# Sums over the key blocks behind: block sums by VectorE, 18 products a head in place of 20

## The reference, cut to what matters

```
z = einsum('bhqd,bhkd->bhqk', q_blk, k32) * scale
mask = key_pos[None, :] < q_pos[:, None]
log_1m_beta = where(mask, log_sigmoid(-z), 0.0)
stick = cumsum(log_1m_beta, axis=3, reverse=True) - log_1m_beta
att = where(mask, exp(log_sigmoid(z) + stick), 0.0)
out = einsum('bhqk,bhkd->bhqd', att, v32)
```

## Time and profile before

| | |
|---|---|
| median of three executions | 1718.95 us |
| profiled execution, its own time | 1719.79 us |
| its span in the profile | 1717.8 us |
| TensorE busy | 1692.4 us, 99% |
| VectorE busy | 1316.4 us, 77% |
| ScalarE busy | 778.2 us, 45% |
| GpSimd busy | 780.0 us, 45% |
| mean granted TensorE clock | 0.998 |

### The profile page before, as it was taken

The page is one execution under the profiler, slowest core; times in us unless marked ns, Lnnn a source line. Parts: engine busy times, 40 slices in busy tenths (PEclk is TensorE's granted clock), DMA queues, the critical chain, the costliest instruction groups (busy, mean ns, idle before and its releaser), DMA issues.

```text
span 1717.8 us, 24432 instructions
## 1 busy us (share of the span) xinstructions
PE 1692.4 (99%) x9073; PEld 1511.4 (88%) x9073; DVE 1316.4 (77%) x1872; ACT 778.2 (45%) x1124; POOL 780.0 (45%) x494
## 2 busy tenths in 40 slices
PE   7999999999999999999999999999999999999998
PEld 6878788878899999999999999999888888888886
DVE  4666622265889999989999777766778888888887
ACT  4445433344333666656666566654323323323233
POOL 4333243333702556655656667770453433433430
PEclk9999999999999999999999999999999999999999
DMA  5222223332335677686776977788999999999992
GB/s 159 74 73 85 61 86 98 89 85 84 111 112 207 233 250 256 232 303 242 245 258 240 346 273 269 271 298 306 378 352 396 383 382 391 380 372 390 385 390 90
DMA packets 212443, 413.88 MB, mean 241 GB/s; under 512 B 11520, under 2 KB 150816, under 8 KB 207008
## 3 DMA queue, kind: packets, MB, share of 16 engines
q1 hardware_dynamic: 156880, 253.51, 42.4%
q0 software_dynamic: 36864, 134.23, 21.4%
q10 hardware_dynamic: 18640, 25.45, 4.2%
HBM read 360.73 MB, written 52.43 MB: 241 GB/s over the span
## 4 chain that ended last, share of the span: by engine, by line
PE 87%; DVE 9%; ACT 2%; issue 1%; DMA 0%; ACTq 0%; SPq 0%; DVEq 0%
PE psum L1371 30%; PE psum L1312 25%; PE psum L284 20%; PE psum L1302 4%; PE psum L1339 2%; DVE ul L1567 2%; DVE ring L1642 1%; PE psum L358 1%; PE psum L512 1%; DVE hot L1630 1%; PE psum L345 1%; PE psum L372 1%; DVE hot L1632 1%; DMA acc<-in_x 0%; PE psum L327 0%
## 5 line engine op out<-in xcount | busy, mean ns | idle before, releaser
L1312 PE MATMUL psum<-xnTh,uh 128*128 128x384 f32 x1024 | 354.2, 346 | 3.4 <-DVE ul L1567 2.6
L1312 PE MATMUL psum<-xnTh,ul 128*128 128x384 f32 x1024 | 343.4, 335 | 0.0
L1312 PE MATMUL psum<-xnTl,uh 128*128 128x384 f32 x1024 | 343.4, 335 | 0.0
L236 POOL TENSOR_TENSOR wl<-raw,wh 128x1024 fp32r<-128x1024 f32 x72 | 177.1, 2465 | 280.4 <-ACT wh L586 279.9
L1371 PE MATMUL psum<-vh,dwh 128*128 128x512 f32 x768 | 298.8, 389 | 0.2 <-DVE dwl L1660 0.2
L1371 PE MATMUL psum<-vh,dwl 128*128 128x512 f32 x768 | 298.8, 389 | 0.0
L1371 PE MATMUL psum<-vl,dwh 128*128 128x512 f32 x768 | 298.8, 389 | 0.0
L1526 POOL DMA_INDIRECT ring<-in_expert_v,index x128 | 172.1, 1345 | 251.7 <-DVE acc L1647 208.1
L1444 ACT ACTIVATE vh<-v_raw 128x4096 fp32r<-128x4096 f32 x31 | 112.7, 3634 | 339.2 <-PE psum L1371 338.7
L1526 POOL DMA_INDIRECT ring<-in_expert_u,index x128 | 169.7, 1326 | 181.0 <-DVE ring L1642 107.8
L1642 DVE SCALAR_TENSOR_TENSOR ring<-ring,x 128x1024 f32<-128x1024 f32 x128 | 197.1, 1559 | 5.0 <-issue 2.9
(11 more groups left out here) (230 smaller groups left out, 3029.3 us busy)
## 6 DMA issues: line engine op xcount, KB each, us to landing
u_raw<-in_expert_u SPq DMA_DIRECT2D x128, 512.0 KB
v_raw<-in_expert_v SPq DMA_DIRECT2D x30, 2048.0 KB, 14.0
expert_act<-hb ACTq DMA_DIRECT2D x128, 192.0 KB
expert_gate<-grid SPq DMA_DIRECT2D x12, 2048.0 KB, 6.9
dh<-expert_act SPq DMA_DIRECT2D x32, 768.0 KB
dg<-expert_gate SPq DMA_DIRECT2D x32, 768.0 KB
raw<-in_w_in SPq DMA_DIRECT2D x40, 512.0 KB, 3.9
raw<-in_w_q SPq DMA_DIRECT2D x16, 512.0 KB, 4.0
```

Of the source, the lines that this page charges most:

```text
L236: nc.gpsimd.tensor_tensor(wl[slot][:], raw[slot][:], wh[slot][:].bitcast(F), ALU.subtract).then_inc(w_lo[slot], 1)
L1312: last = nc.tensor.matmul(zb[s][:, 0:DT], w[s][:, c, :], x[:, c, 0:DT], start=(c == 0 and i == 0), stop=(c == C - 1 and i == 2))
```

## The change

For each head VectorE adds three blocks: `sx[0]` is key block 2 plus key block 3 for the queries of block 3, `sx[1]` is key block 1 plus key block 2 for the queries of block 2, and `sx[2]` is key block 1 plus `sx[0]` for the queries of block 3. ScalarE copies the high part of these 384 columns (`sxh`), and VectorE subtracts the low part (`sxl`). TensorE multiplies the block right behind a key block by ones as before, and what lies further behind as one product on the summed blocks. The counts of the semaphore `vmax` go from one to three for each head.

```diff
+    sx = m.put("sx", 84, [P, 2, 3, P])
+    sxh = m.put("sxh", 87, [P, 2, 3, P], R)
+    sxl = m.put("sxl", 90, [P, 2, 3, P], R)
...
             pe.wait_ge(S["t_used"], p * 2 + e + PRIMED)
+            blocks = [[part[:, e, ROW[kb]:ROW[kb] + T - kb * P] for kb in range(NB)] for part in (sph, spl)]
+            behind = [part[:, e, :, :].rearrange("p n q -> p (n q)") for part in (sxh, sxl)]
             for kb, o in ROW.items():
-
-                for jb in range(kb, NB):
-                    for half in (sph, spl):
-                        last = nc.tensor.matmul(
-                            zt[o // T][:, o % T + (jb - kb) * P:o % T + T - kb * P], (tri_r if jb == kb else ones_r)[:],
-                            half[:, e, ROW[jb]:ROW[jb] + T - jb * P], start=(jb == kb and half is sph),
-                            stop=(jb == NB - 1 and half is spl))
+                o0, at = o // T, o % T
+                for own, sums_ in zip(blocks, behind):
+                    first, final = own is blocks[0], own is blocks[1]
+                    nc_out = zt[o0][:, at:at + T - kb * P]
+                    last = nc.tensor.matmul(nc_out, tri_r[:], own[kb], start=first, stop=(final and kb == NB - 1))
+                    if kb < NB - 1:
+                        last = nc.tensor.matmul(zt[o0][:, at + P:at + 2 * P], ones_r[:], own[kb + 1][:, 0:P], start=False,
+                                                stop=(final and kb == NB - 2))
+                    if kb < NB - 2:
+                        rest = sums_[:, 0:P] if kb == 1 else sums_[:, P:3 * P]
+                        last = nc.tensor.matmul(zt[o0][:, at + 2 * P:at + T - kb * P], ones_r[:], rest, start=False, stop=final)
             last.then_inc(S["t_full"], 1)
...
         def softplus_hi(p, e):
             act.wait_ge(S["sp_ready"], p * 2 + e + 1)
+            nc.scalar.activation(sxh[:, e, :, :], sx[:, e, :, :], ACT.Copy)
             nc.scalar.activation(sph[:, e, :], sp[:, e, :], ACT.Copy).then_inc(S["sp_hi"], 1)
...
-            dve.wait_ge(S["vmax"], p * 2 + e + 1)
+            n0 = (p * 2 + e) * 3
+            dve.wait_ge(S["vmax"], n0 + 1)
 
             for part in diagonals(sp, e):
                 last = nc.vector.tensor_tensor(part, part, wide(causal), ALU.mult)
-            last.then_inc(S["sp_ready"], 1)
+            last.then_inc(S["vmax"], 1)
+            dve.wait_ge(S["vmax"], n0 + 2)
+            b1, b2, b3 = (sp[:, e, ROW[kb]:ROW[kb] + T - kb * P] for kb in (1, 2, 3))
+            nc.vector.tensor_tensor(sx[:, e, 0, :], b2[:, P:2 * P], b3, ALU.add).then_inc(S["vmax"], 1)
+            nc.vector.tensor_tensor(sx[:, e, 1, :], b1[:, P:2 * P], b2[:, 0:P], ALU.add)
+            dve.wait_ge(S["vmax"], n0 + 3)
+            nc.vector.tensor_tensor(sx[:, e, 2, :], b1[:, 2 * P:3 * P], sx[:, e, 0, :], ALU.add).then_inc(S["sp_ready"], 1)
 
         def soft_lo(p, e):
             dve.wait_ge(S["sp_hi"], p * 2 + e + 1)
+            nc.vector.tensor_tensor(sxl[:, e, :, :], sx[:, e, :, :], sxh[:, e, :, :].bitcast(F), ALU.subtract)
             nc.vector.tensor_tensor(spl[:, e, :], sp[:, e, :], sph[:, e, :].bitcast(F), ALU.subtract).then_inc(S["sp_lo"], 1)
```

## The result

The changed kernel takes 1729.64 us (median of 6 runs, 1727.79 to 1732.81), the kernel before 1719.12 us (6 runs, 1717.53 to 1720.37). The ratio is 1.0065 with a 95% interval of 1.0055 to 1.0075: 10.5 us slower. Forecast were 1730.4 us, in a range of 1725.0 to 1735.5.

What follows compares the result with a forecast made beforehand. The prediction took the VectorE and ScalarE chain, with 0.1 us of TensorE slack, as the bound: 9.1 us of delay over four pairs plus 2.4 for the clock, 11.5 over the median 1718.95, gives 1730.4 us, range 1725.0 to 1735.5.

Steps and rivals of the forecast that it cites:

- The bound: Attention stage: VectorE and ScalarE form one chain from softplus to L871, and TensorE has 0.1 us of slack to it.
- The chain's move: In each pair, spl of head 1 and everything behind it on VectorE, including L871 of head 0, come 2.55 us later.
- soft of head 1: Pair 1, VectorE: L855 of head 1 starts 0.93 us later, using up the 0.62 us of idle time before it.
- adds: VectorE, ahead of sp_ready: three adds of 128 columns lengthen the chain by 0.71 us per head.
- sxh: ScalarE, ahead of sph: the high copy of 384 columns takes up 0.43 us per head.
- sxl: VectorE, ahead of spl: the low part of 384 columns takes 0.47 us of engine time per head.
- The pairs: Delay paid once per pair: 2.1 us in the first, 2.2 in the next two, 2.55 in the last; 9.1 in all.
- The stalls: TensorE idles 1.0 us before project(1) and 1.9 before sums of head 1, in each of three pairs.
- TensorE's saving: Sums: fewer, smaller products save 0.36 us a head, 2.9 us for 8 heads; none of it counts in the last pair.
- The clock: New stalls before sums of head 1 may drop TensorE to 1.2 GHz, 1.6 us each; 2.4 us taken, bounds 0 to 4.8.
- The exclusion between VectorE and GpSimd: wcol's copy and GpSimd's split exclude each other; the order stays, so wcol ends 2.55 us later.
- the fourth rival: wcol comes before GpSimd's split, so VectorE regains 2.1 to 2.3 us in each pair: 1718.9 us; 6 in 100.

Runs made afterwards that it cites:

- the filled kernel: The changed kernel plus unused 512-column products in TensorE's stalls, 6 before the sums of head 1 and 8 in the last pair's stall: 1726.45 us.
- e1_products_only: Against the kernel before: only TensorE's 18 products, without the adds, sxh and sxl, reading columns of sph and spl instead: ratio 1.0001.
- The fills: Unused products put into TensorE's stalls: in the changed kernel 1726.45 us; in the kernel before, 7 in the last pair's stall, 1717.30 against 1719.06 us.
- e2_work_only: The changed kernel with the 20 old products in sums, all added work done but its result unused: median 2.7 us above the changed kernel.
- e3_adds_only: The kernel before, 20 products, plus the three adds per head ahead of sp_ready, without sxh and sxl: 1724.95 us, 6.1 above before.
- e4_off_chain: The changed kernel's work reordered: sp_ready right behind the masks, adds later, sxh behind sph, sxl behind spl: median 5.3 us over the kernel before.
- the early subtraction: Head 0's subtraction moved inside the convolution, in reordered kernels: 1719.09 us with 18 products, 1722.24 with 20 and no block sums, beside 1719.06 before.

## Why the prediction was right

- **The bound.** VectorE's chain to the subtraction of head 0, with 0.1 us of slack, was read rightly; the waits appear where they were named.
- **The chain's move.** Forecast 2.55 us, measured 2.49 (25.59 against 23.10). Its terms: 0.93 to soft of head 1 (measured 0.91), adds 0.71 (0.73: ScalarE's copy starts 0.76 behind the masks' end, where it was 0.03), sxh 0.43 (0.44), sxl 0.47 (0.47).
- **The pairs.** Forecast 2.1, 2.2 and 2.2; outputs moved by 2.06 in pair 0 (35.21 against 33.15) and 2.17 in pair 2, and in pair 1 by 2.17 in the filled kernel, where no fall hides it. The last: forecast 2.55, measured 2.44 (the first product with cvh starts 32.09 after cb, 29.65 before). The sum is 8.8 against 9.1.
- **The stalls.** Forecast 1.0 and 1.9 us, measured 0.8 and 1.7. The view counts from the recorded end of a product, 0.16 behind the time when the next could start, so by the starts it is 1.0 and 1.8 (159.83 to 161.90, less 0.23). There are four places, not three: the last pair has both stalls too, ahead of its longer one. The last wait grew by 0.32, from 1.85 to 2.17; 0.36 was forecast, TensorE's own saving.
- **TensorE's saving.** 0.36 us a head by the loads, and of no use in the last pair, as forecast. With the chain left as it was, 1.1 of the 2.9 us came through (e1_products_only).
- **The clock.** Forecast 2.4 us with bounds from 0 to 4.8; 10.5 less 8.8 leaves 1.7. This is a difference of medians, not a measured term. The fills took 2.6 to 3.2 us off the changed kernel (beside before or as it stands) and 1.8 off before, not clear of noise, which gives 0.8 to 1.4. The price of one fall is 1.53 us in pair 1 (36.95 against 35.42 in pair 2), forecast 1.6. That the sum came near is partly luck, since the number of falls was a choice (half of three) and the picture of before was off: I took its one fall as given and the new ones as extra. The two profiles have one fall each. Of the stalls of 1.3 to 1.7 us before the sums of head 1 (four each in the changed kernel, e2_work_only, e3_adds_only and e4_off_chain) 3 of 16 show a fall. Of the unfilled last stalls, 1.8 to 2.2 us, 5 of 9 do (e2_work_only left out, where the clock was already low); the changed kernel's, though longer than before's, does not. So a fall at such a stall comes in some executions and not in others, in before too.
- **The exclusion between VectorE and GpSimd** kept its order, as argued against the fourth rival: the split starts 0.97 us before spl's end, forecast 1.0. The rule that the prediction takes from the Trainium skill, as told there, is for VectorE instructions with two inputs in SBUF. The copy to wcol has one input, so it is no example of it; that such a copy is held too is what the runs show (2.34 us in place of 0.16). The example with two inputs is sxl, 2.16 in place of 0.56. And I missed its best use: that it is also where added work costs nothing.
- **Everything behind the attention** moved as a whole: from the first product with ath to the end are 1507.3 us before and 1507.9 after.

## What to carry to other kernels

Read the slack of the bounding engine to the chain beside it, in the timelines, before work is handed over: here VectorE was 64% busy in the stretch of pair 1, and with 0.1 us of slack, 1.2 us of its time and 0.4 of ScalarE's for each head cost 10.5 us in all. The same change gains 2 to 3 us if that work stands in the idle time between a request and its answer, or takes the place of an operation that GpSimd would hold off anyway. Moving an operation can cost more than it frees when it brings others against GpSimd's, as the early subtraction did. So each move is to be followed to the next meeting with the other engine.

## What the runs showed of the hardware

- A copy of four columns took 0.16 us where nothing held it and 2.34 beside a subtraction of GpSimd. An operation with two inputs in SBUF was held in the same way (sxl 2.16 in place of 0.56), one that reads PSUM was not (cz 0.69 beside the same split). With GpSimd's splits back to back, VectorE's operations got in one at a time between them: two folds took 3.24 us when the first met the end of a split, and 4.89 when it met one just begun.
- Stalls of 1.7 to 2.2 us are followed by the clock's lower level (granted clock 0.50) in some executions and not in others. A fall cost 1.5 to 1.6 us where a profile without it stands beside. One in e2_work_only lasted longer than the others, from 209.5 to 219.7 us with another stall inside, and cost about 3.8 (an estimate: the last pair from cb to ath is 42.64 us there and 38.87 with the fill). None of the four profiles with unused products in the last stall shows a fall in the attention, and three of the ten without them show none either. That unused products keep the clock up is therefore likely, but not proven.
- The first cb, at the end of the part ahead of the attention, starts up to 4.2 us later in one profile than in another; what depends on it is best measured from there.
